# Block attention: five of eight rotary rotations done by transfers in place of permutation products

## The reference, cut to what matters

```
qkv = (x @ w_qkv)                      # 1024 -> 3 x 16 heads x 64
def apply_rope(t, cos, sin):
    t1, t2 = split(t, 2, axis=-1)      # halves of 32 channels of each head
    return concatenate([t1 * cos - t2 * sin, t2 * cos + t1 * sin], axis=-1)
q = apply_rope(q, cos, sin) * 64 ** -0.5
k = apply_rope(k, cos, sin)
out = softmax(causal(q @ k.T)) @ v @ w_o
```

## Time and profile before

| | us |
|---|---|
| median of 3 runs | 1288.02 |
| lowest, highest | 1287.43, 1288.23 |
| the profiled execution, its own time | 1287.18 |
| its span, first to last instruction | 1285.4 |
| TensorE matmuls busy | 1240.1 (96%) |
| VectorE busy | 899.6 (70%) |
| ScalarE busy | 640.4 (50%) |

### The profile page before, as it was taken

How to read it: one execution, slowest core, us unless ns; L and a number is a source line. 1 busy time by engine, 2 the same in 40 slices (tenths; PEclk the granted TensorE clock), 3 DMA queues, 4 the chain that set the end, 5 groups by cost and what they waited for, 6 DMA issues and landing times.

```text
span 1285.4 us, 22079 instructions
## 1 busy us (share of the span) xinstructions
PE 1240.1 (96%) x9364; PEld 1085.7 (84%) x9364; DVE 899.6 (70%) x1433; ACT 640.4 (50%) x966; POOL 69.8 (5%) x43
## 2 busy tenths in 40 slices
PE   6999999999999999999999989999999999999997
PEld 4788998888888898778888879999898977788886
DVE  7456886766665677666665568989999766666555
ACT  3443446554444545655445545343455556655553
POOL 0022000002000051000100010000000000000000
PEclk9999999999999999999999999999999999999999
DMA  9542202775655373327565546455544443365550
GB/s 324 150 130 85 81 4 91 234 235 184 203 184 185 127 243 122 131 87 242 182 201 184 188 144 204 129 181 180 164 132 164 139 156 120 113 208 186 193 180 33
DMA packets 156355, 206.36 MB, mean 161 GB/s; under 512 B 9952, under 2 KB 129888, under 8 KB 156128
## 3 DMA queue, kind: packets, MB, share of 16 engines
q1 hardware_dynamic: 156256, 204.94, 48.2%
HBM read 202.83 MB, written 1.05 MB: 159 GB/s over the span
## 4 chain that ended last, share of the span: by engine, by line
PE 72%; DVE 19%; ACT 7%; issue 2%; DMA 0%; DVEq 0%; SPq 0%; ACTq 0%
PE PS L599 15%; PE PS L551 11%; PE PS L552 11%; PE PS L553 11%; PE PS L604 8%; DVE WW L2190 6%; PE PS L972 4%; DVE PH L2800 4%; ACT WW L1544 2%; PE PS L903 1%; DVE PA L2436 1%; PE PS L943 1%; ACT Xb L1583 1%; PE PS L676 1%; DVE PH L2818 1%
## 5 line engine op out<-in xcount | busy, mean ns | idle before, releaser
L2190 DVE TENSOR_TENSOR WW<-RG,WW 128x2048 fp32r<-128x2048 f32 x164 | 381.0, 2337 | 141.3 <-ACT WW L1544 141.1
L1544 ACT ACTIVATE WW<-RG 128x2048 fp32r<-128x2048 f32 x164 | 311.2, 1907 | 25.2 <-PE PS L553 24.4
L599 PE MATMUL PS<-AHL,WW 128*128 128x512 f32 x864 | 216.9, 392 | 0.5 <-DVE WW L2190 0.5
L551 PE MATMUL PS<-AHL,WW 128*128 128x256 f32 x704 | 203.3, 289 | 2.6 <-DVE AHL L2236 1.8
L552 PE MATMUL PS<-AHL,WW 128*128 128x256 f32 x704 | 199.1, 283 | 0.0
L553 PE MATMUL PS<-AHL,WW 128*128 128x256 f32 x704 | 199.1, 283 | 0.0
L599 PEld LDWEIGHTS PS<-AHL,WW 128*128 128x128 f32 x864 | 157.0, 189 | 30.1 <-DVE WW L2190 0.9
L551 PEld LDWEIGHTS PS<-AHL,WW 128*128 128x128 f32 x704 | 134.9, 192 | 5.3 <-issue 3.7
L552 PEld LDWEIGHTS PS<-AHL,WW 128*128 128x128 f32 x704 | 135.0, 192 | 1.7 <-issue 1.4
L553 PEld LDWEIGHTS PS<-AHL,WW 128*128 128x128 f32 x704 | 134.9, 192 | 0.0
L604 PEld LDWEIGHTS PS<-AHL,WW 128*128 128x128 f32 x864 | 118.4, 190 | 8.8
(11 more groups left out here) (375 smaller groups left out, 1825.3 us busy)
## 6 DMA issues: line engine op xcount, KB each, us to landing
RG<-in_ffn_w_in SPq DMA_DIRECT2D x44, 1024.0 KB, 5.2
RG<-in_w_ff SPq DMA_DIRECT2D x32, 1024.0 KB, 5.5
RG<-in_w_in SPq DMA_DIRECT2D x30, 1024.0 KB, 5.2
RG<-in_ffn_w_down SPq DMA_DIRECT2D x22, 1024.0 KB, 4.9
RG<-in_w_rkv SPq DMA_DIRECT2D x12, 1024.0 KB, 6.5
RG<-in_moba_w_qkv SPq DMA_DIRECT2D x12, 1024.0 KB, 6.5
RG<-in_w_o SPq DMA_DIRECT2D x4, 1024.0 KB, 7.9
RG<-in_wx_kv SPq DMA_DIRECT2D x4, 1024.0 KB, 5.5
```

Source lines behind the costliest of these rows:

```text
L551: e.matmul(o, lh, rh, start=start, stop=False)
L599: e.matmul(PS[b][:, :].rearrange("p (a t) -> p a t", a=2), wh, AHL[:, :, k * 256:k * 256 + 256], start=k == 0, stop=False)
L1544: s.activation(WH[hi_n % NW], ring(SPLIT[hi_n]), ACT.Copy, bias=0.0, scale=1.0).then_inc(s_hi, 1)
L2190: v.tensor_tensor(WL[lo_n % NW], ring(SPLIT[lo_n]), WH[lo_n % NW].bitcast(F32), ALU.subtract).then_inc(s_lo, 1)
```

## The change

Five rotations (units 2 to 6) are no longer permutation products. SP issues four transfers for each, which copy the swapped halves of 32 partitions from `raw` into `rot`, two buffers in the upper half of `Xb`; VectorE multiplies from `rot`. Since a copy cannot change a sign, the sign moves from the permutation matrix into the table of sines. Units 0, 1 and 7 keep their products. On SP's queue the rotation of unit 2 stands behind the last key piece (`mk3s`), those of units 3, 4 and 5 each behind one output-weight piece (`mo0`, `mo1`, `mo2`), that of unit 6 behind the first piece of the feed-forward layer. Each has a wait for `raw` in front. TensorE waits before units 4 to 7 for the copy to `raw` of the unit four before (and before 4 and 5 for its rotation as well). ScalarE's copy of unit 0 gets a wait for the layer norm's remainder, and its rounding of the third chunk of the output a wait for all eight rotations, since `Xb` is used before and after.

```
--- before.py
+++ after.py
@@ -58,7 +58,7 @@
     put('sel2', (p // 64) == np.arange(2)[None, :])
     n_out, n_in = f % 64, p % 64
     same = (p // 64) == (f // 64)
-    put('perm', np.where(same & (n_out < 32) & (n_in == n_out + 32), -1.0, 0.0)
+    put('perm', np.where(same & (n_out < 32) & (n_in == n_out + 32), 1.0, 0.0)
         + np.where(same & (n_out >= 32) & (n_in == n_out - 32), 1.0, 0.0))
     t1 = np.arange(256)[None, :] - 128
     ok = np.concatenate([f <= p, t1 <= p], 1)
@@ -67,7 +67,7 @@
     inv = (np.float32(10000.0) ** (-np.arange(0, 64, 2, dtype=np.float32) / np.float32(64))).astype(np.float32)
     ang = np.arange(T, dtype=np.float32)[None, :] * inv[:, None]
     put('cos', np.tile(np.cos(ang), (4, 1)))
-    put('sin', np.tile(np.sin(ang), (4, 1)))
+    put('sin', np.where(p64 < 32, -1.0, 1.0) * np.tile(np.sin(ang), (4, 1)))
     return a
 
 
@@ -213,6 +213,7 @@
         s_fc, s_fa = sem("ffn_small"), sem("ffn_summed")
         s_fg, s_fx, s_fhh, s_fhl, s_dn = (sem(n) for n in ("ffn_gate", "ffn_prod", "ffn_hi", "ffn_lo", "ffn_down_mm"))
         s_rw, s_rc, s_pm, s_rp, s_v2 = (sem(n) for n in ("rope_raw", "rope_cos", "rope_mm", "rope_out", "moba_v"))
+        s_rot = [sem(f"rope_rotated{n}_in") for n in range(2)]
         s_sc, s_mx, s_ex, s_pn, s_pt, s_pta, s_pv, s_oa = (sem(n) for n in (
             "score_mm", "score_max", "exped", "probs", "probsT_mm", "probsT", "pv_mm", "head_out"))
         s_sg, s_ub, s_tap, s_pad, s_tap0 = (sem(n) for n in ("conv_sig", "conv_in", "conv_taps", "conv_pad", "conv_first"))
@@ -358,6 +359,7 @@
         OT = take(2048).rearrange("p (k t) -> p k t", k=8)
         raw = [take(512) for _ in range(2)]
         rc = [take(512) for _ in range(2)]
+        rot = [Xb[:, 1024 + 512 * n:1536 + 512 * n] for n in range(2)]
         TMP = take(3072)
         OTf = OT.rearrange("p k t -> p (k t)")
         cosb = cst('cos').unsqueeze(1).broadcast_to([128, 2, 256])
@@ -430,6 +432,12 @@
                 for dst, src in parts:
                     d.dma_start(dst(ring(name)), src).then_inc(s_ring[SLOT[name]], 16)
 
+            def rotate(u):
+
+                d.wait_ge(s_rw, u + 1)
+                for o_, i_ in ((0, 32), (32, 0), (64, 96), (96, 64)):
+                    d.dma_start(rot[u % 2][o_:o_ + 32, :], raw[u % 2][i_:i_ + 32, :]).then_inc(s_rot[u % 2], 16)
+
             def gains(name, g_, b_):
                 piece(name, (lambda r: r[:, 0:1024], g_.broadcast_to([128, 1024])),
                       (lambda r: r[:, 1024:2048], b_.broadcast_to([128, 1024])))
@@ -439,6 +447,8 @@
                     if j < n:
                         for u, un in enumerate(units):
                             piece(f'f{f}{un}{j}', wcols(w_in, u * 256 * n + 256 * j, 256))
+                            if (f, j, u) == (1, 0, 0):
+                                rotate(6)
                         if j == 1 and f < 2:
                             if f == 0:
                                 d.wait_ge(s_yy, 8)
@@ -500,10 +510,14 @@
                 if j == 3:
                     piece('mv2s', wcols(M, 2560, 512, 0, 4))
                     piece('mv3s', wcols(M, 2560, 512, 4, 4))
-                piece(f'mq{j}', wcols(M, 256 * j, 256))
-                piece(f'mk{j}s', wcols(M, 1024 + 256 * j, 256))
+                for u in range(2):
+                    piece(f'mk{j}s' if u else f'mq{j}', wcols(M, 1024 * u + 256 * j, 256))
+                if j == 3:
+                    rotate(2)
             for n in range(4):
                 piece(f'mo{n}', wcols(a['moba_w_o'], 512 * (n % 2), 512, 4 * (n // 2), 4))
+                if n < 3:
+                    rotate(3 + n)
             piece('mvA', wcols(a['wx_kv'], 512, 256))
             ffn(1, 11, 'gu', a['ffn_w_in'][1], a['ffn_w_down'][1])
             piece('mvB', wcols(a['wx_kv'], 768, 256))
@@ -1286,26 +1300,23 @@
                     token_piece('mv2s', 7, 1, 0)
                     split_ready('mv3s')
                     token_piece('mv3s', 6, 0, 1)
-                    rope_turn(5)
                     token_piece('mv3s', 7, 1, 1)
                 for u, name in ((2 * j, f'mq{j}'), (2 * j + 1, f'mk{j}s')):
                     split_ready(name)
                     stepping = u in (3, 4, 5, 6, 7)
                     if u == 3:
                         e.wait_ge(s_v2, 2)
-                    if u == 4:
-                        e.wait_ge(s_rp, 1)
+                    if u in (4, 5):
+                        e.wait_ge(s_rp, u - 3)
                     if u == 6:
                         e.wait_ge(s_v2, 3)
                     if u == 7:
                         e.wait_ge(s_v2, 4)
                     if u >= 4:
-                        e.wait_ge(s_rp, u - 3)
+                        e.wait_ge(s_rw, u - 3)
                     chan_piece(name, 4 + u % 4, 0)
                     if stepping:
                         step()
-                        if u != 6:
-                            rope_turn(u - 1)
                     chan_piece(name, 4 + u % 4, 1)
                     if stepping:
                         step()
@@ -1953,6 +1964,8 @@
                 piece_done(name)
                 if u >= 2:
                     s.wait_ge(s_rp, u - 1)
+                if u == 0:
+                    s.wait_ge(s_tl, H_AT['ln1'] + 4)
                 s.activation(raw[u % 2], PS[4 + u % 4][:, :], ACT.Copy, bias=0.0, scale=1.0).then_inc(s_rw, 1)
 
             def moba_v(h, banks, name, half_mm):
@@ -1991,6 +2004,7 @@
             ahead('mo1')
             turned_heads(A1, heads + 2)
             s.wait_ge(s_oa, 6)
+            s.wait_ge(s_rp, 8)
             rounded(OTf, (2,), 1.0, XH)
             exped(A1, heads + 2)
             attention(A1, heads + 3)
@@ -2724,8 +2738,13 @@
 
             def rope_turned(u):
                 d_ = (QQ, KK)[u % 2][:, 2 * (u // 2):2 * (u // 2) + 2, :]
-                v.wait_ge(s_pm, u + 1)
-                own_dve(v.tensor_tensor(d_, PS[4 + u % 4][:, :].rearrange("p (m t) -> p m t", m=2), sinb, ALU.mult))
+                if u in (0, 1, 7):
+                    v.wait_ge(s_pm, 3 if u == 7 else u + 1)
+                    src = PS[4 + u % 4][:, :]
+                else:
+                    v.wait_ge(s_rot[u % 2], 64 * ((u - 2) // 2) + 64)
+                    src = rot[u % 2]
+                own_dve(v.tensor_tensor(d_, src.rearrange("p (m t) -> p m t", m=2), sinb, ALU.mult))
                 own_dve.done()
                 v.wait_ge(s_rc, u + 1)
                 v.tensor_tensor(d_, d_, rc[u % 2].rearrange("p (m t) -> p m t", m=2), ALU.add).then_inc(s_rp, 1)
```

12 lines of the change are left out of this document (6 added, 6 removed).

## The result

| | before | after |
|---|---|---|
| median of 6 runs, us | 1287.46 | 1292.30 |
| lowest, highest | 1287.39, 1288.23 | 1291.46, 1293.43 |
| ratio of the times | | 1.0036 [1.0025, 1.0047] |
| span of the profiled execution | 1285.4 | 1290.7 |

The change makes the kernel slower by 4.8 us, or 0.36% (interval 0.25% to 0.47%). The forecast was 1288.8 us, 0.75 us above the median of 1288.02 that it started from, and its range ended at 1290.6; the measured time lies above it.

The account below looks back on a forecast made before the run. The prediction took a ring of ScalarE and VectorE work (8.96 us a turn) to bound units 3 to 5, and TensorE the stretch from 498.89 to 521.5. +1.6 - 0.86 = +0.75 us gave 1288.8 us, range 1286.7 to 1290.6.

Parts of the forecast that it names:

- +0.75: Sum for the whole kernel: +1.6 us for unit 2's late landing, less 0.86 us for unit 5's product.
- Units 3 and 4: nothing lost, 0.13 won once: Their transfers land in time; a TensorE copy no longer late for ScalarE's exponential gains 0.13 us once.
- Unit 5: -0.86: Its removed product stood where TensorE has no idle time, so removal saves 0.86 us.
- Unit 2: +1.6, the landing at 483.8: Transfers queued behind mk3s land at 483.8, making VectorE 1.75 us late; less 0.13, 1.6 us at 498.89.
- 256 KB put between the two land at 483.1 + 0.65: Unit 2's transfers, between mk3s and mo0 in the queue, land 0.65 us after mk3s, at about 483.8.
- Rival 2: At VectorE's unit 2 wait, transfers take 0.62 us each, landing from 485.6 on: +2.6 to +3.6 us; chance 0.13.
- Unit 6: "Worth nothing" and "Cost nothing": Removing its product gains nothing, as VectorE ends the idle time before 531.72; its transfers land with 0.65 us to spare.
- TensorE's idle time growing from 0.40 to about 4.6 us: Between 484 and 501 us, TensorE's idle time grows by 2.6 and 1.6 us to about 4.6 us.
- about 3.2 us: VectorE's wait for a transfer at unit 2's multiplication, starting near 480.7, with none at units 3 to 6.

Follow-up runs that it names:

- r2_half: The changed kernel with only two of unit 2's four transfers, half of that unit's rotated values left out; one run, 1292.61 us.
- only_r6: The kernel before with unit 6 alone rotated by transfers, all other units by products; 1290.35 us, ratio 1.0018.
- r6_product: The changed kernel with unit 6's rotation as a permutation product again, units 2 to 5 by transfers; 1290.26 us, ratio 1.0018.
- pool_waits: The changed kernel with GpSimd's cosine product of unit 7 waiting for VectorE's first remainder of the output; 1291.82 us, ratio 1.003.
- r2_product: The changed kernel with unit 2's rotation as a product again, units 3 to 6 by transfers; 1290.54 us, ratio 1.0021.
- r26_product: The changed kernel with units 2 and 6 as products again, units 3, 4 and 5 by transfers; 1288.58 us, ratio 1.0003.
- pe_busy_pool: The changed kernel with unread products in TensorE's two idle times (three, then two before the output projection) and the GpSimd wait of pool_waits; 1290.98 us.
- pe_busy: The changed kernel with three unread products ahead of the scores of heads 4 and 5 and three ahead of the output projection; 1291.28 us, ratio 1.0027.
- only_r5: The kernel before with unit 5 alone rotated by transfers; 1286.92 us, ratio 0.9994.
- r2_ahead: The changed kernel with unit 2's transfers queued ahead of weight pieces mq3 and mk3s, and unit 6 by product; 1288.15 us, ratio 1.0001.

## Why the prediction was wrong

The sign of its sum was right, and so was the shape at unit 2: TensorE waits for VectorE, VectorE for the transfers. Its +0.75 falls short of the profiles' +4.8 (5.3 less the 0.57 ahead of the block) by three terms: 1.4 us of unit 2's landing, 1.1 of the output's first remainder and 1.6 of the clock. Step by step:

1. **Units 3 and 4: nothing lost, 0.13 won once.** Right. The landings were in time, and the 0.13 can be read: from one remainder of weights to the next it is 9.06 us in before (484.07 to 493.13) and 8.94 in after (487.73 to 496.67).
2. **Unit 5: -0.86.** Right: -0.89 in the profile, and -0.89 in the profile of unit 5 alone. (That "each of the 16 recorded passes is 592 ns long" is true of the median alone, they run from 590 to 697; no term of the sum hangs on it.)
3. **Unit 2: +1.6, the landing at 483.8.** Mis-sized: +2.97. The steps behind the landing hold: from the multiplication to the next remainder it is 1.99 us (485.74 to 487.73), as the sum had it (483.85 to 485.8). It is the term for the landing that failed. In the time of before's profile (less 0.57) it came at 485.2, so 1.4 us later than 483.8. "256 KB put between the two land at 483.1 + 0.65" took the rate of 1024 KB pieces; they took 1.15. And it took 483.1 for mk3s as given, where mk3s moved by 0.9. Rival 2 had "a landing at 485.6" and +2.6 to +3.6 at this place, which is near to what came, but not by its mechanism: at 0.62 us a transfer, half of them would have taken off 1.2 us, and r2_half took off 0.65. That would have been luck, and its 1291.6 us at the far end is still below the measured time.
4. **Unit 6: "Worth nothing" and "Cost nothing".** This step failed outright, by 2.5 us (only_r6: +2.4; r6_product against after: -2.5). The landing was in time as forecast, at 529.9 for a multiplication at 530.8. What failed is that the text costed the removal of work in front of a wait at nothing, and named VectorE as what ends the wait, without asking what else the earlier finish would trigger. Unit 7's copy came 0.05 us earlier against the remainders, GpSimd's product overtook VectorE's remainder, and that cost 1.1 (shown by the durations in the profiles, and by pool_waits, where the remainder takes its old time).
5. **The clock, which is in no step.** The forecast foresaw TensorE's idle time growing from 0.40 to about 4.6 us; it was 3.43 + 0.83 = 4.3. It gave that no price. Behind the 3.43 us, and behind the 3.13 us at the output projection, the granted clock went to 0.50. At the first place that cost next to nothing in after, since TensorE still waited 0.83 us at 502.43. At the second it cost 1.6 us. From the first product of the output projection to the next scores it is 6.66 to 6.72 us in the three profiles whose clock went down there (after, r2_half, r2_product), and 5.07 to 5.15 in the eleven others. The stretch behind the scores of heads 6 and 7 says the same: to the next scores it is 17.8 us in the three profiles whose clock went down there (r2_product, r26_product, pe_busy_pool), and 16.3 in the nine others that have no product in it.

The profile's other forecasts (six passes, VectorE waiting at unit 2 for "about 3.2 us", no wait at 3 to 6) came out but for the size: 4.44 us.

Three things stay open. Why the small transfers cost the DMA engines more time for a byte was not settled. When the clock goes down was not either. It went down behind 2.00, 2.31, 3.13 and 3.43 us of idle time, but not behind the 3.13 of only_r6, the 2.31 of pe_busy and the 2.03 of pool_waits. It also went down in places that no edit touches and where before's profile has the same idle time at 1.00: in only_r5 at 1062 us behind 1.37 us, in r6_product at 1100 us behind 1.40. So part of the spread of every kernel here is the clock's, and one profile doesn't tell how often it falls. And issuing unit 2's transfers from another engine's queue was not tried; the DMA engines were busy throughout at that time (371 GB/s from 471 to 480 us), so whether it would help is open.

## What to carry to other kernels

Work taken from an engine that waits anyway isn't free of consequences: write down how long the engine then stands idle, what its earlier finish triggers on every other engine, and what those meet. In some executions the granted clock fell behind an idle time of TensorE, here of 1.4 to 3.4 us, and where TensorE then sets the pace that cost about 1.6 us; a few matmuls nobody reads can be cheaper than such an idle time, and of the products removed here only the one in the stretch that TensorE bounds was worth more than 0.13 us. Small transfers queued behind a saturated queue of loads cost more here than their bytes at the loads' rate (1.15 us in place of 0.65), and the loads in front of them and behind them landed later too.

## What the runs showed of the hardware

- An issue on a backed-up queue can hold up SP: the first transfer of unit 2 took 2.79 us to issue, the next 0.59. In r2_ahead, with two weight pieces fewer in front, the first took 0.59, and the piece mo0 behind them 2.47. The chain of after has the first two (start, duration, what):

```profile
473.88 2.79 SPq L439
476.71 0.59 SPq L439
```

- SBUF-to-SBUF transfers of 64 KB in 2 KB rows took 0.29 us each behind a full queue of loads. The piece behind them moved by more: mo0 landed 15.4 us after the copy to `raw` started, in place of 13.0.
- Of the four transfers, the counts of the first three are reached 9.7 to 10.3 us after the start of that copy, ahead of mk3s at 11.3, and the fourth at 12.5. The four share one semaphore. The Trainium skill (DMA: Bandwidth & Descriptors, "Why a DMA increments its semaphore by 16 and not by 1") says that each DMA engine adds its own count, so that a count reached with several transfers in flight on one semaphore doesn't tell that the first has landed. The rows here look like that, though nothing run here proves it; VectorE waits for the whole sum, so it makes no difference to the kernel.
- Which of two engines starts 0.02 to 0.05 us earlier decided between 0.68 and 1.79 us for the operation of VectorE that meets one of GpSimd (before, after).
